# First attention: turning the probabilities with VectorE blocks and copies on the chip, in place of TensorE transposes

## The chip, the cores and the metric

The kernel runs on one core of one Trainium2 chip. The metric is the device time of one execution in microseconds. All five compute engines of the core run instruction streams of their own and meet at semaphores, written by hand.

## What is computed

Two blocks of a network run one behind the other on 256 tokens of 2048 features, all in float32. The first block has an attention layer with a relative bias (phase A), then one with forget gates (phase B), each with 32 heads of 128. The second block is a hybrid of convolution, sliding window attention and a recurrence, and the change does not touch it. The core of both phases, cut from the reference (bias, decay and masks in one name here):

```python
h = rms_norm(x, norm)
q, k, v, g = projections of h             # each 256 x 4096, 32 heads of 128
sc = einsum('bqhd,bkhd->bhqk', q, k) * scale + bias_or_decay_and_mask
p = softmax(sc)
o = einsum('bhqk,bkhd->bqhd', p, v)
x = x + (o * silu(g)) @ w_out
```

## The kernel before

**Tiling.** Tokens are taken in two halves of 128. Queries of the first half see the keys of the first half only (in both phases), queries of the second half see all 256 keys. So one head has 128x128 and 128x256 scores, 384 columns, and `scores` holds two heads: 128 partitions (queries) by 768. Two heads are a pair; each phase has 16 pairs, the first and the last written out, the 14 between in a loop.

**Weights.** Each product with a weight matrix goes in units of 256 columns: four units a pair (q, k, v, g), then 16 units for the output projection of the phase. A unit has four chunks (`PIECES`). SyncE loads a chunk of 512 KB to `w_raw` (`load_unit`, line 489), ScalarE rounds it to `w_hi` (`split_hi`, 685), VectorE makes the rest `w_lo` (`split_lo`, 1812), and TensorE multiplies with both (`multiply`, 1290; its matmuls are L1306 and L1308). `w_raw` and `w_both` each hold one unit. So SyncE may load a chunk when VectorE has split the same chunk of the unit before, ScalarE may split it when TensorE has used the same chunk of the unit before, and TensorE has three chunks to work through in between. Line 496 is the load, 689 the ScalarE split, 1814 the VectorE split.

**One pair,** in the order of TensorE (`pair`, 1356): unit k, unit v, the scores (1379, 1380), unit g, then six transposes (1387) of the finished probabilities into `ps_t`, the unit q of the next pair, and then `values(n)` (1394), which multiplies `v_tok` with the turned probabilities `p_t`. ScalarE copies `ps_t` to `p_t` (795). In the last pair of a phase `values` is not called there, but in the output projection, behind the first chunk of its first unit (`halves`, 1467, with `first_wait` at `s == 1`, 1474).

VectorE (`pair`, 1901) adds the bias to the scores (1921), splits chunk 0 of the next unit, takes the row maxima, splits chunk 1, waits for ScalarE's exponentials (784), scales by the reciprocal sums (1936, four instructions, then `p_ready`), and splits chunks 2 and 3. Further on it takes `g_t`, splits the next unit, takes `q_t` of the next pair (`take_scaled`) and multiplies the heads by the gate (`gate_heads`, 1958). In the last pair it splits parts of the gated heads in between (1896).

SyncE (`load_pair`, 511) loads the units in order, each chunk behind its wait, with one bias load (526) a pair ahead of unit v. In the second block it also makes copies from SBUF to SBUF (574, 585), all on the same queue.

The order on each engine is the order of the code. Nothing is planned by a tool.

Of the kernel before, what the change touches and what calls it, by code (L numbers as in the profile page):

```python
# [11 lines left out]
ACT = mybir.ActivationFunctionType  # L12
AX_X = mybir.AxisListType.X

P = 128
D = 2048
KT = D // P
S = 256
# [3 lines left out]
HEADS = INNER // P  # L22
PAIRS = HEADS // 2
UNIT_N = 256
PIECES = 4
PK = KT // PIECES
OUT_ORDER = ((0, 0), (0, 1), (0, 2), (1, 0), (0, 3), (1, 1), (1, 2), (1, 3))
QKVG = 4
OUT_N = D // UNIT_N
# [143 lines left out]
def build_program(nc, io, const_at):  # L173
    with ExitStack() as ctx:
# [3 lines left out]
        def sem(name):  # L178
            return ctx.enter_context(nc.semaphore(name))
# [7 lines left out]
        scratch = sb("scratch", [P, 18680])  # L187
# [3 lines left out]
        ps_s = ctx.enter_context(nc.psum_tensor("ps_s", [P, 2, 512], F32))  # L191
        ps_t = ctx.enter_context(nc.psum_tensor("ps_t", [P, 2, 512], F32))
        cum_dram = nc.dram_tensor("cumulative_log_forget", (HEADS, S), F32).ap()

        ident, ones = consts[:, 0:P], consts[:, P:2 * P]
# [8 lines left out]
        one = Region(scratch)  # L204
# [4 lines left out]
        bias_raw = one.take(2, S)  # L209
        bias = one.take(2, 384)  # L210
        scores = one.take(2, 384)
        p_t = one.take(2, 384)
        v_tok = one.take(2, S)
        tanh_g = one.take(2, S)
        sumsq = one.take(2, S)
# [8 lines left out]
        row_max = one.take(2, 2)  # L224
        row_sum = one.take(2, 2)

        before = p_t.rearrange("p a b -> p (a b)")
        vec_rows = before[:, 0:P]
        gate, gate_t, gate_u = (before[:, P + 2 * HEADS * n:P + 2 * HEADS * (n + 1)]
                                .rearrange("p (t h) -> p t h", t=2) for n in range(3))  # L230
        fw = og.rearrange("p h s -> p (h s)")[:, 3 * D:3 * D + KT * HEADS].rearrange("p (k h) -> p k h", k=KT)
        cum_row = bias.rearrange("p a b -> p (a b)")[0:HEADS, 0:S]
        squares = g_t
        first_squares = [g_t, v_t]
        z_rows = scores.rearrange("p a b -> p (a b)")[0:2 * HEADS, 0:2 * S]
# [72 lines left out]
        sides = [operand[:, n * SIDE:(n + 1) * SIDE].rearrange("p (k n) -> p k n", n=RAW_T) for n in range(4)]  # L308
# [53 lines left out]
        exp_done = sem("exp_done")  # L362
        recip_ready = sem("recip_ready")
        p_ready = sem("p_ready")
        turned = sem("turned")
        pt_ready = sem("pt_ready")
        tanh_done = sem("tanh_done")
        silu_ready = sem("silu_ready")
        o_done = sem("o_done")
# [100 lines left out]
        w_out_of = {"A": io["a_w_out"][0], "B": io["b_w_out"][0]}  # L470
# [15 lines left out]

        @block.sync
        def _(sp):
            def load_unit(unit, w, row0, column):

                for s in range(PIECES):

                    sp.wait_ge(pieces_split, unit * PIECES + s + 1)
                    rows = w[row0 + s * PK * P:row0 + (s + 1) * PK * P, :]
                    src = rows.rearrange("(k p) n -> p k n", p=P)[:, :, bass.ds(column, UNIT_N)]
                    sp.dma_start(w_raw[:, s], src).then_inc(raw_landed[s], 16)
# [11 lines left out]
            sp.dma_start(fw, io["f_w"].rearrange("(k p) n -> p k n", p=P)).then_inc(consts_in, 16)  # L508
            sp.dma_start(fb, io["f_b"].rearrange("(a n) -> a n", a=1).to_broadcast([P, HEADS])).then_inc(consts_in, 16)

            def load_pair(phase, i, last, first=False):
                unit = UNIT0[phase] + QKVG * i
                n = pair0[phase] + i

                if first:
                    load_unit(unit + 2, w_of[phase][2], 0, i * UNIT_N)
                    sp.wait_ge(cum_copied, 1)
                    sp.dma_start(cum_dram, cum_row).then_inc(cum_stored, 16)
                    sp.wait_ge(cum_stored, 16)
                sp.wait_ge(bias_ready, n + 1)  # L520
                if phase == "A":
                    rb = io["a_rel_bias"]
                    src = bass.AP(rb.tensor, rb.offset + 2 * i * REL + (REL - 2 * S + P), [[1, P], [REL, 2], [1, S]])
                else:
                    src = bass.AP(cum_dram.tensor, 2 * i * S, [[0, P], [S, 2], [1, S]])
                sp.dma_start(bias_raw, src).then_inc(bias_landed, 16)
                for c in (3,) if first else (2, 3):
                    load_unit(unit + c, w_of[phase][c], 0, i * UNIT_N)
                if not last:
                    for c in (0, 1):  # L530
                        load_unit(unit + QKVG + c, w_of[phase][c], 0, (i + 1) * UNIT_N)

            for phase in phases:
                if phase == "B":
                    for c in (0, 1):
                        load_unit(UNIT0[phase] + c, w_of[phase][c], 0, 0)
                load_pair(phase, 0, False, first=phase == "B")
                with sp.Fori(1, PAIRS - 1) as i:
                    load_pair(phase, i, False)
                load_pair(phase, PAIRS - 1, True)  # L540
                with sp.Fori(0, OUT_N) as j:
                    for half in range(2):
                        load_unit(UNIT0[phase] + UNITS_ATT + 2 * j + half, w_out_of[phase], half * D, j * UNIT_N)

# [136 lines left out]
        def _(act):  # L681
# [75 lines left out]
            def pair(phase, i, last, first=False):  # L757
                n = pair0[phase] + i
                unit = UNIT0[phase] + QKVG * i
                output = OUTPUT0[phase] + QKVG * i  # L760

                for s in range(PIECES):
                    split_hi(unit + 2, s)
                    if first and phase == "A" and s == 2:
                        root_of(0)
                copy_half(unit + 1, output + 1, 1)

                for s in range(PIECES):
                    split_hi(unit + 3, s)
                act.wait_ge(proj_free, output + 4)  # L770
                if first:
                    act.wait_ge(rstd_ready, phases.index(phase) + 1)
                scale_half_values(unit + 2, 0)

                if last:
                    gated_hi(pair0[phase], 0)
                split_hi(unit + 4, 0)
                if last:
                    gated_hi(pair0[phase], 1)
                split_hi(unit + 4, 1)  # L780
                act.wait_ge(negmax_ready, n + 1)
                for h in range(2):
                    for t, (a, b) in enumerate(((0, P), (P, 384))):
                        act.activation(scores[:, h, a:b], scores[:, h, a:b], ACT.Exp, bias=row_max[:, t, h:h + 1],
                                       accum_out=row_sum[:, t, h:h + 1]).then_inc(exp_done, 1)
                split_hi(unit + 4, 2)
                if last:
                    gated_hi(pair0[phase], 2)
                split_hi(unit + 4, 3)
                if last:  # L790
                    gated_hi(pair0[phase], 3)
                copy_half(unit + 3, output + 3, 1)

                act.wait_ge(turned, n + 1)
                act.activation(p_t, ps_t[:, :, 0:384], ACT.Copy).then_inc(pt_ready, 1)
                act.wait_ge(scaled, 3 * n + 3)
                act.activation(tanh_g, g_t, ACT.Tanh).then_inc(tanh_done, 1)
                if not last:
                    for s in range(PIECES):
                        split_hi(unit + 5, s)  # L800
                    copy_half(unit + 4, output + 4, 0)
# [485 lines left out]
        def _(pe):  # L1287
# [68 lines left out]
            def pair(phase, i, last, first=False):  # L1356
# [24 lines left out]
                m.then_inc(scores_done, 1)  # L1381
                multiply(unit + 3, 1, h_q)

                pe.wait_ge(p_ready, n + 1)
                for h in range(2):
                    for c in range(3):
                        m = pe.transpose(ps_t[:, h, c * P:(c + 1) * P], scores[:, h, (0, P, 2 * P)[c]:(0, P, 2 * P)[c] + P], ident)  # L1387
                m.then_inc(turned, 1)
                if not last:
                    pe.wait_ge(proj_free, output + 5)  # L1390
                    multiply(unit + 4, 0, h_q)
                    values(n)

            def values(n):
                pe.wait_ge(pt_ready, n + 1)
                for h in range(2):
                    pe.matmul(ps_s[:, h, 0:S], v_tok[:, h, 0:P], p_t[:, h, 0:S], start=True, stop=False)  # L1397
                    m = pe.matmul(ps_s[:, h, P:S], v_tok[:, h, P:S], p_t[:, h, S:384], start=False, stop=True)  # L1398
                m.then_inc(o_done, 1)

            def gates():
# [403 lines left out]
        def _(dve):  # L1805
# [6 lines left out]
            def split_lo(unit, s):  # L1812
                dve.wait_ge(hi_ready, unit * PIECES + s + 1)
                dve.tensor_tensor(w_lo[:, s], w_raw[:, s], w_hi[:, s].bitcast(F32), ALU.subtract).then_inc(pieces_split, 1)  # L1814
# [19 lines left out]
            def take_scaled(output, bank, dst, scale=1.0):  # L1834

                take_output(output, bank, dst)
                dve.wait_ge(proj_free, output + 3)
                scale_by_rstd(dst, scale)
# [62 lines left out]
            def pair(phase, i, last, first=False):  # L1901
# [32 lines left out]
                for h in range(2):  # L1934
                    for t, (a, b) in enumerate(((0, P), (P, 384))):
                        m = dve.tensor_scalar(scores[:, h, a:b], scores[:, h, a:b], row_sum[:, t, h:h + 1], None, ALU.mult)
                m.then_inc(p_ready, 1)
                if last:
                    gated_lo(phases.index(phase), 1)
                split_lo(unit + 4, 2)  # L1940
# [11 lines left out]
                if not last:  # L1952
                    for s in range(1, PIECES):
                        split_lo(unit + 5, s)
                    take_scaled(output + 4, 0, q_t, scale=SCALE)
                    gate_heads(n, 2 * i)

# [701 lines left out]
```

## Time and profile before

| | us |
|---|---|
| three runs, median | 2716.82 |
| lowest and highest | 2714.08, 2718.45 |
| span of the profiled execution | 2712.8 |

The profile is one execution with the times of each instruction. Busy time is the union of an engine's instructions; matmuls overlap each other, since they are pipelined. SPq is SyncE's queue of DMA issues, and the duration of a row there is the issue, not the movement of the data. PEclk is the clock that TensorE was granted, as a share of 2.4 GHz.

| engine | busy us | share |
|---|---|---|
| TensorE | 2692.7 | 99% |
| VectorE | 1810.4 | 67% |
| ScalarE | 1399.0 | 52% |
| GpSimd | 141.5 | 5% |

### The profile page before, as it was taken

To read this page: it belongs to the slowest core of one execution; us is meant where nothing else is said; L and a number is where in the kernel's file an instruction comes from. 1 tells how busy PE (TensorE), PEld (TensorE's weight loads), DVE (VectorE), ACT (ScalarE), POOL (GpSimd) and SP (SyncE) were. 2 spreads that over 40 slices of the span, in tenths; PEclk is the share of its full clock that TensorE was granted. 3 is DMA by queue.
4 is the path that set the end of the run, shared out by engine and by line. 5 is a ranking of instruction groups with operands and counts; after the bars stand their busy time and mean duration, and the time that the engine had idled before them with its cause. 6 is when DMAs were issued, how large, how long until landed. Compare 5 with 4: busy or idle time off the path is not lost.

```text
span 2712.8 us, 45296 instructions
## 1 busy us (share of the span) xinstructions
PE 2692.7 (99%) x17061; PEld 2415.2 (89%) x17061; DVE 1810.4 (67%) x2380; ACT 1399.0 (52%) x2132; POOL 141.5 (5%) x138
## 2 busy tenths in 40 slices
PE   8999999999999999999999999999999999999998
PEld 7888888888888888888888888888999999999987
DVE  7566565665665576565565656755889886689776
ACT  6444444444454454444444444544565774566764
POOL 0000000000000001001010010000000000000000
PEclk9999999999999999999999999999999999999999
DMA  7656666565556656565556565566554445564463
GB/s 228 184 177 184 178 181 177 179 185 175 178 177 191 188 160 184 176 181 178 178 181 182 178 180 177 176 191 188 182 170 147 133 153 172 166 184 149 133 208 127
DMA packets 474106, 475.94 MB, mean 175 GB/s; under 512 B 18090, under 2 KB 469058, under 8 KB 473730
## 3 DMA queue, kind: packets, MB, share of 16 engines
q1 hardware_dynamic: 473748, 474.35, 57.4%
q8 instruction: 70, 1.15, 0.2%
q14 instruction: 32, 0.26, 0.0%
q10 hardware_dynamic: 256, 0.18, 0.0%
HBM read 470.53 MB, written 2.13 MB: 174 GB/s over the span
## 4 chain that ended last, share of the span: by engine, by line
PE 93%; DVE 5%; ACT 1%; issue 1%; DMA 0%; SPq 0%; ACTq 0%; DVEq 0%
PE proj L1306 34%; PE proj L1308 17%; PE proj L1321 9%; PE proj L1493 6%; PE proj L1495 6%; PE proj L1494 6%; PE proj L1323 4%; PE proj L1715 2%; PE ps_s L1397 1%; DVE w_both L2152 1%; PE ps_s L1380 1%; DVE scratch L2311 1%; PE proj L1717 1%; PE ps_t L1387 1%; PE ps_s L1398 1%
## 5 line engine op out<-in xcount | busy, mean ns | idle before, releaser
L1306 PE MATMUL proj<-operand,w_both 128*128 128x512 f32 x3968 | 1402.5, 398 | 1.7 <-issue 1.2
L1814 DVE TENSOR_TENSOR w_both<-w_raw,w_both 128x1024 fp32r<-128x1024 f32 x644 | 799.4, 1244 | 694.1 <-ACT w_both L689 693.0
L689 ACT ACTIVATE w_both<-w_raw 128x1024 fp32r<-128x1024 f32 x644 | 681.8, 1059 | 916.7 <-PE proj L1308 704.4
L1308 PE MATMUL proj<-operand,w_both 128*128 128x256 f32 x4096 | 1143.4, 279 | 0.0
L1306 PEld LDWEIGHTS proj<-operand,w_both 128*128 128x128 f32 x3968 | 745.1, 188 | 175.5 <-issue 1.6
L1308 PEld LDWEIGHTS proj<-operand,w_both 128*128 128x128 f32 x4096 | 772.9, 189 | 0.8
L1493 PE MATMUL proj<-operand,w_both 128*128 128x272 f32 (+2 forms) x1540 | 448.6, 291 | 0.1
L1494 PE MATMUL proj<-operand,w_both 128*128 128x272 f32 (+2 forms) x1540 | 442.6, 287 | 0.0
L1495 PE MATMUL proj<-operand,w_both 128*128 128x272 f32 (+2 forms) x1540 | 442.4, 287 | 0.0
L1321 PE MATMUL proj<-w_both,operand 128*128 128x512 f32 x1024 | 363.2, 399 | 0.0
L2152 DVE TENSOR_TENSOR w_both<-w_raw,w_both 128x1024 fp32r<-128x1024 f32 x226 | 275.0, 1222 | 124.9 <-ACT w_both L902 124.0
L902 ACT ACTIVATE w_both<-w_raw 128x1024 fp32r<-128x1024 f32 x226 | 236.9, 1054 | 175.7 <-PE proj L1495 137.9
L1493 PEld LDWEIGHTS proj<-operand,w_both 128*128 128x128 f32 x1540 | 290.5, 189 | 5.7 <-issue 3.3
L1494 PEld LDWEIGHTS proj<-operand,w_both 128*128 128x128 f32 x1540 | 291.3, 189 | 0.3
L1495 PEld LDWEIGHTS proj<-operand,w_both 128*128 128x128 f32 x1540 | 291.4, 189 | 0.0
L1323 PE MATMUL proj<-w_both,operand 128*128 128x256 f32 x1024 | 287.6, 281 | 0.0
L1321 PEld LDWEIGHTS proj<-w_both,operand 128*128 128x128 f32 x1024 | 192.5, 188 | 47.7
L1323 PEld LDWEIGHTS proj<-w_both,operand 128*128 128x128 f32 x1024 | 193.7, 189 | 0.0
L2311 DVE SCALAR_TENSOR_TENSOR scratch<-scratch 128x272 f32<-128x272 f32 (+1 forms) x240 | 102.1, 487 | 0.8
L1715 PE MATMUL proj<-w_both,operand 128*128 128x512 f32 x224 | 79.4, 397 | 0.9 <-DVE w_both L2152 0.9
L1818 DVE TENSOR_TENSOR scratch<-proj,scratch 128x512 f32<-128x512 f32 x110 | 75.1, 683 | 0.1
L1831 DVE SCALAR_TENSOR_TENSOR scratch<-scratch 128x512 f32<-128x512 f32 x96 | 66.5, 693 | 3.3
(374 smaller groups left out, 2143.1 us busy)
## 6 DMA issues: line engine op xcount, KB each, us to landing
w_raw<-in_a_w_in_dram SPq DMA_DIRECT2D x256, 512.0 KB, 3.7
w_raw<-in_w_in_dram SPq DMA_DIRECT2D x160, 512.0 KB, 3.6
w_raw<-in_b_w_in_dram SPq DMA_DIRECT2D x128, 512.0 KB, 3.7
w_raw<-in_kv_w_dram SPq DMA_DIRECT2D x128, 512.0 KB, 3.8
w_raw<-in_a_w_out_dram SPq DMA_DIRECT2D x64, 512.0 KB, 4.6
w_raw<-in_b_w_out_dram SPq DMA_DIRECT2D x64, 512.0 KB, 4.1
w_raw<-in_w_out_dram SPq DMA_DIRECT2D x64, 512.0 KB, 3.6
scratch<-in_a_rel_bias_dram SPq DMA_DIRECT2D x16, 256.0 KB, 3.8
```

Of the source, the lines that this page charges most:

```text
L689: act.activation(w_hi[:, s], w_raw[:, s], ACT.Copy).then_inc(hi_ready, 1)
L902: act.activation(w_hi[:, s], w_raw[:, s], ACT.Copy).then_inc(hi_ready, 1)
L1306: pe.matmul(proj[:, 2 * bank + t, :], w_hi[:, s, kk, cols], rhs[:, k, :], start=first and k == 0, stop=False)
L1308: m = pe.matmul(proj[:, 2 * bank + t, 0:S], w_lo[:, s, kk, cols], rhs[:, k, 0:S], start=False, stop=last and end)
L1321: pe.matmul(proj[:, 2 * bank + t, :], hi, w_both[:, s, kk].rearrange("p a n -> p (a n)"), start=k == 0, stop=False)
L1323: m = pe.matmul(proj[:, 2 * bank + t, 0:UNIT_N], lo, w_hi[:, s, kk, :], start=False, stop=k == KT - 1)
L1493: pe.matmul(out, w_hi[:, s, kk, cols], hi, start=first, stop=False)
L1494: pe.matmul(out, w_hi[:, s, kk, cols], lo, start=False, stop=False)
L1495: return pe.matmul(out, w_lo[:, s, kk, cols], hi, start=False, stop=last)
L1715: pe.matmul(proj[:, bank + t, :], y[0][:, k, tokens], w_both[:, s, kk].rearrange("p a n -> p (a n)"), start=k == 0, stop=False)
L1814: dve.tensor_tensor(w_lo[:, s], w_raw[:, s], w_hi[:, s].bitcast(F32), ALU.subtract).then_inc(pieces_split, 1)
L2152: dve.tensor_tensor(w_lo[:, s], w_raw[:, s], w_hi[:, s].bitcast(F32), ALU.subtract).then_inc(pieces_split, 1)
```

## The change

The six transposes on TensorE and ScalarE's copy from PSUM go. VectorE turns the 128x768 probabilities in blocks of 32x32 (`p_blocks`, which lies on `q_t` and half of `k_t`, both read by then): a block stays in its own group of 32 partitions. Sixteen copies from SBUF to SBUF, of 32 partitions by 192 numbers (24 KB) each, move the blocks to the partitions of their keys (`p_keys`, in the place and size of `p_t`). They are issued by SyncE, eight ahead of the load of chunk 2 of the unit after the next pair's q and eight ahead of chunk 3. TensorE's `values` waits for all 16 to land and reads `p_keys` in runs of 32 numbers. VectorE waits for the same before it overwrites `q_t`. In the last pair of a phase the unit loaded among the copies is the second of the output projection, whose first two units move from the loop to here.

```diff
-        p_t = one.take(2, 384)
+        p_keys = one.take(4, 6, 32)
+        p_blocks = scratch[:, HEADS * S:HEADS * S + 768].rearrange("p (b c j) -> p b c j", b=4, c=6)
...
+            def move_blocks(n, sides):
+                sp.wait_ge(p_blocked, n + 1)
+                for b in sides:
+                    for a in range(4):
+                        sp.dma_start(p_keys[32 * b:32 * b + 32, a], p_blocks[32 * a:32 * a + 32, b]).then_inc(p_landed, 16)
...
-                if not last:
-                    for c in (0, 1):
-                        load_unit(unit + QKVG + c, w_of[phase][c], 0, (i + 1) * UNIT_N)
+                if last:
+                    following = [(w_out_of[phase], half * D, 0) for half in range(2)]
+                else:
+                    following = [(w_of[phase][c], 0, (i + 1) * UNIT_N) for c in range(2)]
+                load_unit(unit + QKVG, *following[0])
+                load_unit(unit + QKVG + 1, *following[1], chunks=(0, 1))
+                move_blocks(n, (0, 1))
+                load_unit(unit + QKVG + 1, *following[1], chunks=(2,))
+                move_blocks(n, (2, 3))
+                load_unit(unit + QKVG + 1, *following[1], chunks=(3,))
...
-                with sp.Fori(0, OUT_N) as j:
+                with sp.Fori(1, OUT_N) as j:
...
-                act.wait_ge(turned, n + 1)
-                act.activation(p_t, ps_t[:, :, 0:384], ACT.Copy).then_inc(pt_ready, 1)
...
-                pe.wait_ge(p_ready, n + 1)
-                for h in range(2):
-                    for c in range(3):
-                        m = pe.transpose(ps_t[:, h, c * P:(c + 1) * P], scores[:, h, (0, P, 2 * P)[c]:(0, P, 2 * P)[c] + P], ident)
-                m.then_inc(turned, 1)
...
-                pe.wait_ge(pt_ready, n + 1)
+                pe.wait_ge(p_landed, 256 * n + 256)
                 for h in range(2):
-                    pe.matmul(ps_s[:, h, 0:S], v_tok[:, h, 0:P], p_t[:, h, 0:S], start=True, stop=False)
-                    m = pe.matmul(ps_s[:, h, P:S], v_tok[:, h, P:S], p_t[:, h, S:384], start=False, stop=True)
+                    first = p_keys[:, :, 3 * h:3 * h + 2, :].rearrange("p a c j -> p c a j")
+                    second = p_keys[:, :, 3 * h + 2, :]
+                    pe.matmul(ps_s[:, h, 0:S].rearrange("p (c a j) -> p c a j", c=2, a=4), v_tok[:, h, 0:P], first, start=True, stop=False)
+                    m = pe.matmul(ps_s[:, h, P:S].rearrange("p (a j) -> p a j", a=4), v_tok[:, h, P:S], second, start=False, stop=True)
...
                 m.then_inc(p_ready, 1)
+                dve.wait_ge(p_ready, n + 1)
+                dve.transpose(p_blocks.rearrange("p b c j -> p c b j"),
+                              scores.rearrange("p h (c b j) -> p (h c) b j", c=3, b=4)).then_inc(p_blocked, 1)
...
                     for s in range(1, PIECES):
                         split_lo(unit + 5, s)
+                    dve.wait_ge(p_landed, 256 * n + 256)
                     take_scaled(output + 4, 0, q_t, scale=SCALE)
```

## Rows read from the trace of the kernel before

**Rows 1.** The page: span, TensorE's busy time, its granted clock in 40 slices.

```profile
span 2712.8 us, 45296 instructions
PE 2692.7 (99%) x17061; PEld 2415.2 (89%) x17061; DVE 1810.4 (67%) x2380; ACT 1399.0 (52%) x2132; POOL 141.5 (5%) x138
...
PEclk9999999999999999999999999999999999999999
```

**Rows 2.** TensorE's waits, whole span: total us, times, longest.

```profile
PE proj L1306 <- DVE w_both L1814: 0.5, 2, 0.3
```

**Rows 3.** TensorE in order of time, steady pair: start, us, line, operation.

```profile
544.61 0.28 PE L1308 MATMUL proj<-operand,w_both 128*128 128x256 f32 x1
544.73 0.82 PE L1387 MATMUL ps_t<-consts,scratch 128*128 128x128 f32 x6
...
545.62 0.28 PE L1308 MATMUL proj<-operand,w_both 128*128 128x256 f32 x1
...
545.97 0.28 PE L1308 MATMUL proj<-operand,w_both 128*128 128x256 f32 x1
```

**Rows 4.** The same, where `values` begins.

```profile
556.48 0.59 PE L1397 MATMUL ps_s<-scratch 128*128 128x256 f32 x2
```

**Rows 5.** VectorE in order of time, same pair; idle before and its releaser in brackets.

```profile
535.53 0.95 DVE L1921 TENSOR_TENSOR scratch<-ps_s,scratch 128x768 f32<-128x768 f32 x1
...
542.44 1.01 DVE L1936 TENSOR_SCALAR scratch<-scratch 128x128 f32<-128x128 f32 x4
...
546.02 1.23 DVE L1814 TENSOR_TENSOR w_both<-w_raw,w_both 128x1024 fp32r<-128x1024 f32 x1 [1.44 <-ACT w_both L689]
```

**Rows 6.** ScalarE in order of time, same pair.

```profile
539.38 1.06 ACT L689 ACTIVATE w_both<-w_raw 128x1024 fp32r<-128x1024 f32 x1 [1.71 <-PE proj L1308]
```

**Rows 7.** SyncE's queue of issues, same pair.

```profile
547.41 0.37 SPq L496 DMA_DIRECT2D w_raw<-in_a_w_in_dram  x1
```

**Rows 8.** Issues by line: count, duration ns min/median/max, first and last start.

```profile
L496 SPq DMA_DIRECT2D w_raw<-in_a_w_in_dram x256: 367/373/1721, 3.0 to 764.4; - x128
...
L574 SPq DMA_DIRECT2D scratch<-scratch x40: 624/625/917, 2005.7 to 2451.5; - x40
...
L585 SPq DMA_DIRECT2D scratch<-scratch x8: 607/628/718, 2031.0 to 2424.2; - x8
```

**Rows 9.** SyncE's queue in the second block, in order of time.

```profile
2033.74 0.60 SPq L562 DMA_DIRECT2D w_raw<-in_w_in_dram  x1
...
2045.97 2.94 SPq L574 DMA_DIRECT2D scratch<-scratch  x4
...
2059.52 2.65 SPq L574 DMA_DIRECT2D scratch<-scratch  x4
```

**Rows 10.** Stretches of 0.1 us; last two columns: DMA busy share, GB/s.

```profile
2049.50:2049.60 0.10, 0.10 (x3) 0.10 (x3) 0.10 (x1) 0.10 (x1) 0.00 (x0) 1.00 0.48 87
...
2049.80:2049.90 0.10, 0.10 (x3) 0.10 (x2) 0.10 (x2) 0.10 (x1) 0.00 (x0) 1.00 0.02 0
```

**Rows 11.** DMA issues of the page: size, median us from issue to landing.

```profile
w_raw<-in_a_w_in_dram SPq DMA_DIRECT2D x256, 512.0 KB, 3.7
...
scratch<-scratch SPq DMA_DIRECT2D x8, 136.0 KB, 4.0
...
cumulative_log_forget<-scratch SPq DMA_DIRECT2D x1, 32.0 KB, 1.9
```

**Rows 12.** VectorE and TensorE in order of time, last pair of phase A.

```profile
783.31 1.01 DVE L1936 TENSOR_SCALAR scratch<-scratch 128x128 f32<-128x128 f32 x4
...
789.14 0.67 PE L1397 MATMUL ps_s<-scratch 128*128 128x256 f32 x2
```

**Rows 13.** TensorE at the start in order of time; a stretch, clock third last.

```profile
6.87 1.92 PE L1352 MATMUL ps_t<-consts,scratch 128*128 128x128 f32 x8
...
11.52 1.04 PE L1352 MATMUL ps_t<-consts,scratch 128*128 128x128 f32 x8
...
2700.00:2705.00 5.00, 2.67 (x5) 0.55 (x3) 4.46 (x18) 0.80 (x3) 0.00 (x0) 0.57 0.36 132
```

More of the change, by code:

```diff
@@ L225, in build_program @@
         row_sum = one.take(2, 2)
-        before = p_t.rearrange("p a b -> p (a b)")
+        before = p_keys.rearrange("p a c j -> p (a c j)")
         vec_rows = before[:, 0:P]
@@ L364, in build_program @@
         p_ready = sem("p_ready")
-        turned = sem("turned")
-        pt_ready = sem("pt_ready")
+        p_blocked = sem("p_blocked")
+        p_landed = sem("p_landed")
         tanh_done = sem("tanh_done")
@@ L488, in _, with load_unit @@
         def _(sp):
-            def load_unit(unit, w, row0, column):
-                for s in range(PIECES):
+            def load_unit(unit, w, row0, column, chunks=range(PIECES)):
+                for s in chunks:
                     sp.wait_ge(pieces_split, unit * PIECES + s + 1)
```

## Prediction

> **What bounds the kernel now.** I read the page first: of a span of 2712.8 us TensorE is busy 99%, at a granted clock of nine tenths or more in every slice [rows 1]. Then TensorE's waits: in the matmul lines of the attention loops they come to half a microsecond in all [rows 2]. So TensorE sets the time, and an instruction taken from it is won, as long as nothing it needs comes later than before. Then one steady pair (of 16 in each of the two phases), in order of time, engine by engine, to find how late each input of TensorE may come. Then the queue of SyncE, because all 16 copies are put on it, and last the last pair of a phase, where the code puts `values(n)` elsewhere.
>
> **Removed from TensorE.** Six transposes a pair. Their busy time (0.82 us) overstates them, since matmuls overlap. From the L1308 that starts at 544.61 to the next at 545.62 there are 1.01 us, where two with no transposes between are 0.35 apart (545.62 and 545.97): 0.66 us a pair [rows 3]. Times 32: 21.1 us, 0.78% of the span. This is all that can be won.
>
> **Removed from ScalarE.** One copy of 128x768 a pair. ScalarE otherwise waits for TensorE to free weight buffers (1.71 us ahead of the split at 539.38 [rows 6]), so this is worth nothing.
>
> **Added to VectorE.** One 32x32 block transpose of 128x768 a pair, between the scaling of the probabilities, which starts at 542.44 and takes 1.01 [rows 5], and `split_lo` of chunk 2. No row shows a VectorE transpose. The nearest row of the same size, L1921 on 128x768, took 0.95 us [rows 5]; I take this. The scaling of the same columns in four instructions took 1.01. The ends are 0.7, a quarter less than the nearest row, and 1.9, two passes. The time itself is hidden: `split_lo` of chunk 3 starts only at 546.02, when ScalarE lets it, after 1.44 us of idleness [rows 5], and TensorE uses these chunks three chunks later, of 2.8 us each (from the end of the transposes, 545.3, to 556.48 there are four [rows 3, 4]). It counts only in the chain to `p_landed`.
>
> **Added to SyncE: the issues.** Sixteen copies of 24 KB from SBUF to SBUF. The kernel before has 48 issues of that kind, in the second block. They took 624 to 625 ns (minimum and median of 40, with 8 partitions and 17 KB) and 607 to 628 (of 8, with 64 partitions and 136 KB), against 373 for a weight load of 512 KB [rows 8]. The cost goes by the kind, not by the size, so I take it for 32 partitions too. Ten groups of four stand back to back, 2.65 to 2.94 us each [rows 9]; (2.65 - 0.62) / 3 = 0.675 from one start to the next. A weight load behind such copies took 0.60 instead of 0.37 [rows 9].
>
> **Added: the landing.** The fourth copy of the group at 2045.97 was issued at 2045.97 + 2.94 - 0.62 = 2048.29; after a still moment its packets run from 2049.5 and are gone by 2049.8 [rows 9, 10]. That is 1.5 us from the start of the issue, before the semaphore. The small store of `cum_dram`, 32 partitions and 32 KB, landed after 1.9; the 136 KB copies after 4.0, with weight loads around them [rows 11]. I take 1.8; the ends are 1.5 and 4.0. The last eight copies follow the load of chunk 2 by more than 5 us, so they should find an empty queue.
>
> A page of the Trainium skill, "DMA: Bandwidth & Descriptors", section "Anatomy of one DMA", gives a fixed 2.0 us and bytes/436 GB/s, for the GpSimd path: 2.06 us for 24 KB, an estimate by its figures. By it the sum below would be 0.26 x 32 = 8 us higher; the 1.9 us of the small store [rows 11] lie close to it, and no run here shows that landing for 24 KB; its rules for kernel authors also advise to coalesce anything under 64 KB, which this change does not do.
>
> **The steady pair, summed.** The scaling ends at 543.45; +0.03 allowed for VectorE's wait on its own semaphore, +0.95 transpose, +0.16 until SyncE issues (the split that starts at 546.02 and lasts 1.23 ends at 547.25, the load it releases starts at 547.41 [rows 5, 7]) = 544.59. Eight issues 7 x 0.675 + 0.62 = 5.35, with 0.10 for the first being longer and the gap; the load of chunk 2, 0.65 (its split has long ended); seven starts of 0.675 = 4.73: the last copy starts 10.83 later, at 555.42, and lands at 557.2. Before, `values` started at 556.48 [rows 4]; without transposes TensorE would be there at 555.82. It stands for 1.4 us, and the pair ends 0.77 later than before. The chain repeats in each pair, because its start hangs on TensorE: ScalarE's split at 539.38 was released by TensorE's use of chunk 1 of the same pair's last weight unit [rows 6]. Thirty pairs: +23 us.
>
> **The last pair of each phase.** Its `values` come after one chunk of output weights. Before, they started at 789.14, with the scaling starting at 783.31 and ending 1.01 later at 784.32 [rows 12]. By the same steps the copies land at 784.32 + 0.03 + 0.95 + 0.16 + 10.83 + 1.83 = 798.1, 9.0 us later. Two phases: +18 us. Nothing of this is hidden: the weights are ahead, and TensorE stands in front of them.
>
> **The clock.** Through the attention the page shows nine tenths or more, the 2.4 GHz level [rows 1]; in the closing stretch, where TensorE waits often, it reads 0.57 [rows 13]. At 6.87 us, with next to nothing done on TensorE before, eight transposes took 1.92 us, and eight of the same line 1.04 some 5 us later [rows 13], though the clock column there reads 1.0. So after a stop of 9 to 10 us I expect a few us at half the rate: 0 to 4 us a time, I take 2, so +4 us. After 1.4 us I expect nothing; no row in the loops shows such a stop.
>
> **Moved.** The load of chunk 2 of the following unit is issued some 5 us later (near 550), and chunk 3 at about 556.1, against 547.4 before [rows 7]; behind it wait the bias load and the first loads of the next unit. A weight load lands in about 3.7 us, so at 559.8; ScalarE splits it 3 us later than before, VectorE at about 561. TensorE, now in `values` until 558.5, needs it three chunks later, at 566.8. Some 4.5 us of cover are left; without it each microsecond would cost 32 us. VectorE's new wait for `p_landed` stands ahead of `take_scaled`, `gate_heads` and the next unit's splits; but the split of the late chunk 3, just ahead of it, ends at 562, so this wait comes for free, and `q_t` is not wanted before the next scores. `values` reads its moving operand in runs of 32 elements. No row shows that; with the same count of columns I take nothing (0 to 0.4 us a pair, the upper end if its two 256-column matmuls doubled).
>
> **Sum.** 23 + 18 + 4 = 45 us on the profiled span of 2712.8. That lies 4.0 us below the median of 2716.8 of the runs; the difference is carried along: 2762 us, +1.7%.
>
> **Rivals.** *Cheap issues (faster).* If a 32-partition copy costs what a load costs, 0.42 us from start to start with the gap, the chain from SyncE's first issue is 16 x 0.42 + 0.05 + 1.8 = 8.6 us, the copies land at 553.2, ahead of TensorE at 555.8, and every steady pair gains its 0.66: -20 us. The last pairs still cost 4.9 each, +10. Together -10, 2707 us. It decides below about 0.58 us a start; there the gain of the steady pairs just pays for the last ones. For it speak the issues of the far larger weight loads at 0.37, against it all 48 of the same kind [rows 8].
> *Late landing.* If the copies land after 4.0 us, like the 136 KB ones [rows 11], 2.2 x 32 = 70 us come on top: 2832 us. For it: it is the only landing shown for this kind; against: those were 8 packets an engine among weight loads, these are 2 or so.
> *A balance*, in which issues near 0.58 or two of these terms cancel: no change, 2717.
>
> Page "VectorE: DVE Perf Modes" of the Trainium skill, in "Rules for kernel authors", would give a 128x128 transpose to TensorE where PSUM will do, and calls VectorE fastest only inside 32x32. No time follows from it here; it leans to the slower side.
>
> **How the numbers follow.** Forecast 0.64, late landing 0.10, cheap issues 0.18, balance 0.08. About 0.2% (5 us) can be told from no change, so slower 0.74, same 0.08, faster 0.18. The forecast's own range: landing 1.5 to 2.4 (-10, +19), transpose 0.7 to 1.9 (-8, +30), clock (-4, +4), moving operand (+10 at most): 2740 to 2805. The range for 8 in 10 reaches down to 2706, to the cheap issues, and up to 2815, short of most of the late landing.
>
> **What would show it.** After: no L1387; TensorE idle ahead of the matmuls of `values` about 1.4 us, released by a DMA, 30 times, and about 9 to 10 us twice; SyncE's copies 0.62 us each, 0.675 apart; the last starting 10.8 us after the first. `w_both` waits of TensorE still near none. Wrong if the copies cost near 0.37, if the block transpose is not near 0.95, if TensorE waits for splits (then the moved loads count), or if the matmuls of `values` grow.

## The result and the profile after

The changed kernel takes 2735.6 us (median of 4 runs, 2734.1 to 2739.0) against 2715.7 of the kernel before: ratio 1.0074, 95% interval 1.0061 to 1.0086. The sign was forecast, the size was not: +20 us, not +45. The time lies inside the wide range (2706 to 2815), but below the forecast's own, 2740 to 2805. The span of the profiled execution grew by 22.4 us, from 2712.8 to 2735.2.

From the page of the changed kernel, first the span and the engines, then the chain that ended last:

```profile
span 2735.2 us, 45444 instructions
PE 2686.0 (98%) x16869; PEld 2401.2 (88%) x16869; DVE 1851.5 (68%) x2412; ACT 1378.1 (50%) x2100; POOL 137.3 (5%) x138
...
PE 78%; SPq 8%; DVE 7%; ACT 3%; issue 2%; DMA 2%; ACTq 0%; DVEq 0%
```

TensorE is busy 6.7 us less than before [rows 1], and the kernel is longer. SyncE's queue (SPq) stands in the chain with 8%, where it had nothing. TensorE's waits by line (total, times, longest) say what for; before, there was next to nothing in the attention [rows 2]:

```profile
PE ps_s L1407 <- DMA scratch<-scratch: 27.5, 22, 8.7
...
PE proj L1319 <- DVE w_both L1824: 2.1, 3, 1.7
```

L1407 is the first matmul of `values`. It waits 17.3 us of the 27.5 in two places, the last pairs of the phases, and 2.55 in the first pair. The three waits for split weights, 2.1 us, fall between 13 and 21 us, ahead of the attention's pairs, where the kernel before stops three times too (1.7 us). So the moved loads cost nothing on TensorE.

One steady pair of the changed kernel, in order of time on VectorE, SyncE and TensorE:

```profile
545.72 1.01 DVE L1946 TENSOR_SCALAR scratch<-scratch 128x128 f32<-128x128 f32 x4
546.77 0.98 DVE L1949 STREAM_TRANSPOSE scratch<-scratch 128x768 f32<-128x768 f32 x1
...
547.77 4.96 SPq L517 DMA_DIRECT2D scratch<-scratch  x8
553.00 0.37 SPq L497 DMA_DIRECT2D w_raw<-in_a_w_in_dram  x1
553.42 4.94 SPq L517 DMA_DIRECT2D scratch<-scratch  x8
558.62 0.38 SPq L497 DMA_DIRECT2D w_raw<-in_a_w_in_dram  x1
...
559.62 0.70 PE L1407 MATMUL ps_s<-scratch 128*128 128x256 f32 x2
```

The issues of the copies by their line (ns, minimum, median, maximum), and their landing:

```profile
L517 SPq DMA_DIRECT2D scratch<-scratch x512: 507/591/1513, 64.0 to 1766.1; - x171
...
DMA to landing us min/median/max: 1.7/1.8/3.4
```

The last copy is issued at 553.42 + 4.94 - 0.59 = 557.77 and lands 1.8 us later, at 559.57; `values` starts at 559.62.

**Where the 22.4 us are.** The reciprocal (L1932 before, L1942 after) comes once a pair, so its times measure pairs. Pairs 1 and 15 of phase A and 0 and 15 of phase B; first the kernel before, then the changed one:

```profile
108.89 0.18 DVE L1932 RECIPROCAL scratch<-scratch 128x4 f32<-128x4 f32 x1 [0.53 <-ACT scratch L784]
...
783.10 0.18 DVE L1932 RECIPROCAL scratch<-scratch 128x4 f32<-128x4 f32 x1 [0.53 <-ACT scratch L784]
...
1020.12 0.18 DVE L1932 RECIPROCAL scratch<-scratch 128x4 f32<-128x4 f32 x1 [0.53 <-ACT scratch L784]
...
1742.97 0.18 DVE L1932 RECIPROCAL scratch<-scratch 128x4 f32<-128x4 f32 x1 [0.53 <-ACT scratch L784]
```

```profile
112.49 0.18 DVE L1942 RECIPROCAL scratch<-scratch 128x4 f32<-128x4 f32 x1 [0.53 <-ACT scratch L799]
...
785.60 0.18 DVE L1942 RECIPROCAL scratch<-scratch 128x4 f32<-128x4 f32 x1 [0.53 <-ACT scratch L799]
...
1034.66 0.18 DVE L1942 RECIPROCAL scratch<-scratch 128x4 f32<-128x4 f32 x1 [0.53 <-ACT scratch L799]
...
1753.89 0.18 DVE L1942 RECIPROCAL scratch<-scratch 128x4 f32<-128x4 f32 x1 [0.53 <-ACT scratch L799]
```

| stretch | before | after | difference |
|---|---|---|---|
| start and first pair of A | 108.9 | 112.5 | +3.6 |
| 14 pairs of A | 674.2 (48.16 each) | 673.1 (48.08) | -1.1 |
| end of A to first pair of B | 237.0 | 249.1 | +12.0 |
| 15 pairs of B | 722.9 (48.19) | 719.2 (47.95) | -3.6 |
| from there to the end | 969.8 | 981.3 | +11.5 |

So the steady pairs gain a little, and the two ends cost 23.5 us.

A steady pair falls into two parts. From the reciprocal to the start of `values` the changed kernel takes 14.11 us in nearly every pair, whatever TensorE does: that is the chain through the copies. Before, it was 14.26 and 14.46 in turn, and where nothing waits it is 13.60 or 13.91. From `values` to the next reciprocal TensorE does not wait: 33.82 us in nearly every pair before, between 33.51 and 34.09 after. This second part moves with TensorE's own pace at the same clock (see the last section), not with the copies. So the copies account for a gain of about 0.25 us a steady pair, and the rest of the difference between steady pairs is pace.

At the end of phase A, `values` starts at 799.77, where it started at 789.14 [rows 12]; TensorE's clock by stretches (third last column):

```profile
799.77 1.19 PE L1407 MATMUL ps_s<-scratch 128*128 128x256 f32 x2 [8.64 <-DMA scratch<-scratch]
```

```profile
795.00:800.00 5.00, 0.23 (x1) 0.26 (x2) 1.92 (x2) 2.37 (x3) 0.00 (x0) 0.50 0.37 111
800.00:805.00 5.00, 5.00 (x16) 4.25 (x17) 1.82 (x2) 0.00 (x0) 0.00 (x0) 0.50 0.61 201
805.00:810.00 5.00, 5.00 (x31) 4.42 (x30) 2.16 (x2) 2.48 (x3) 0.00 (x0) 0.98 0.00 0
```

It has waited 8.64 us, and then works five more at the 1.2 GHz level, with 16 matmuls where the next stretch has 31. The clock falls a second time 180 us later, after a wait of only 1.09 us at 984.19 that both kernels have (1.15 before) and that left it alone before. The changed kernel, then the one before at the same work:

```profile
986.00:989.50 3.50, 3.50 (x12) 3.02 (x12) 3.47 (x8) 3.49 (x8) 0.00 (x0) 0.51 0.15 51
```

```profile
973.00:976.50 3.50, 3.50 (x22) 2.92 (x22) 3.47 (x8) 3.49 (x8) 0.00 (x0) 1.00 0.13 46
```

The same matmuls take 1.55 us longer there. It happens again from 2095.4 on, after a wait of 1.75 us (1.72 before), for 1.45 us. The first pair waits 2.55 us, because its exponentials come late and its first eight issues take 5.97 us instead of 4.96: one of them took 1.51. One issue in the loop's first pass took 1.50 too; in the last pairs of the phases, also written out, none did, so what makes an issue long is not shown.

### The profile page after: what moved, and what is told of

It reads as the page before. It is cut to its first block, busy times and chain, and to the rows that moved or that the text cites. A ratio compares the mean times of both kernels' runs of the same rounds, so it can differ in the third digit from the quotient of the medians.

```text
span 2735.2 us, 45444 instructions
## 1 busy us (share of the span) xinstructions
PE 2686.0 (98%) x16869; PEld 2401.2 (88%) x16869; DVE 1851.5 (68%) x2412; ACT 1378.1 (50%) x2100; POOL 137.3 (5%) x138
## 4 chain that ended last, share of the span: by engine, by line
PE 78%; SPq 8%; DVE 7%; ACT 3%; issue 2%; DMA 2%; ACTq 0%; DVEq 0%
PE proj L1319 24%; PE proj L1321 13%; PE proj L1334 9%; SPq L517 8%; PE proj L1503 6%; PE proj L1504 6%; PE proj L1505 6%; PE proj L1336 4%; PE proj L1725 2%; ACT scratch L799 2%; DMA scratch<-scratch 2%; PE ps_s L1407 1%; DVE w_both L2166 1%; PE ps_s L1393 1%; DVE scratch L2325 1%
## 5 line engine op out<-in xcount | busy, mean ns | idle before, releaser
L1841 DVE SCALAR_TENSOR_TENSOR scratch<-scratch 128x512 f32<-128x512 f32 x96 | 72.5, 755 | 3.3
```

## The experiments

Each kernel was timed beside the kernel before on its chip. The medians of the kernel before differ between sittings (2715.0 to 2720.7), so ratios are compared; 0.1% is 2.7 us. Pair lengths are from the reciprocals, as above.

### tail_te: is the loss at the ends of the phases?

```diff
 # TensorE, ScalarE: transposes and copy as before, if last
-                move_blocks(n, (0, 1))
+                if not last:
+                    move_blocks(n, (0, 1), phases.index(phase))
...
-                            values(pair0[phase] + PAIRS - 1)
+                            values(pair0[phase] + PAIRS - 1, r, turned_here=True)
```

> The changed kernel with one thing undone: in the last pair of each phase TensorE turns the probabilities again, and no copies are made there. Theory (a chain of 16 issues that TensorE waits for): each end of a phase cost 11.5 to 12 us in the changed kernel (8.6 and 8.7 us of waiting, and some 3 us at half the clock), so this kernel is 23 us below it: 2712 to 2714 us, within 0.2% of the kernel before. Rival (the cost is spread over all pairs, by late weight loads or by traffic): only a sixteenth of the 20 us comes back, 2734 us.

Measured: ratio 0.9975 (0.9964 to 0.9985), a span of 2712.2. The span is 23 us below that of the changed kernel, as the theory had it, and the spread-out rival is out. But the sum is right in part by luck: the two ends give back 17.7 us (249.1 becomes 239.9, 981.3 becomes 972.8), since TensorE ran the output projections of this kernel at a slower pace, about 3 us each (last section). The other 5.3 come from the start and the steady pairs, whose code is that of the changed kernel; its clock did not fall in the first pair, and more of its pairs ran at the faster pace.

### half_copies: does the number of issues decide?

```diff
-                move_blocks(n, (2, 3))
+                if phase == "A" and isinstance(i, int) and i == 0:
+                    move_blocks(n, (2, 3))
```

> Left out: from the second pair on, the eight copies to partitions 64 to 127, so the second half of the keys works with old numbers. The chain is 8 issues shorter, about 5.6 us. Theory: no steady pair waits any more, so each is 0.66 us shorter than before; the ends of the phases wait about 3 us instead of 8.7 and keep their clock or nearly. Against the kernel before: 28 x -0.66 = -18, ends 2 x (3 - 0.7) = +5, first pair +4, together -9: 2707 us. Rival (the price is that of moved loads or of the block transposes on VectorE, which stay as they are): near the changed kernel, 2730 or more.

Measured: 0.9954 (0.9938 to 0.9971), a span of 2707.0, and every pair after the second at 47.42 us. Its waits for copies:

```profile
PE ps_s L1408 <- DMA scratch<-scratch: 8.7, 3, 3.2
```

Three waits are left, the first pair and the two ends. VectorE's transpose and the copies' place in the queue are as in the changed kernel, so they are not the price.

### unwaited: is anything else paid?

```diff
-                        sp.dma_start(p_keys[32 * b:32 * b + 32, a], ...).then_inc(p_landed, 16)
+                        sp.dma_start(p_spare[32 * b:32 * b + 32, a], ...).then_inc(p_landed, 16)
 # TensorE transposes and works with p_t, as before
```

> Everything that the change adds, and nothing that it removes: VectorE turns the blocks, SyncE makes the 16 copies at the same places (to a spare region), but TensorE still transposes and works with what ScalarE copied from PSUM. TensorE waits for no copy. Theory: all other costs are hidden, so the time is that of the kernel before, 2716 us, or up to 3 us more for the first pairs, whose loads are latest. Rival (moved loads, traffic, VectorE's longer row of work): at least 10 us more than before.

Measured: 0.9993 (0.9983 to 1.0002), a span of 2712.9, pairs of 48.19 and 48.18 us, as before. All that the change adds is hidden, so long as nobody waits for it: the block transpose, 512 issues, the copies' traffic and the late loads.

### shapes: why did an issue take 0.59 and not 0.625?

```diff
+    # phase A, to a spare region; src on q_t and k_t
+    sp.dma_start(dst[to:to + 32, 0:192], src[of:of + 32, 0:192])
+    sp.dma_start(dst[to:to + 8, 192:384], src[of:of + 8, 0:192])
+    sp.dma_start(dst[to:to + 32, 384:928], src[of:of + 32, 0:544])
+    sp.dma_start(dst[to:to + 32, 928:1120], two runs of 96 of src)
```

> TensorE's part is that of the kernel before; nobody waits for the copies, which go to a spare region and serve only to measure the issue. In phase A each group has four forms, one line each: 32 partitions by 192 numbers; 8 by 192; 32 by 544; 32 by two runs of 96. In phase B: 32 by 96; 16 by 192; 32 by 512; 32 by 192. The forecast took 0.625 us an issue from copies of 8 partitions by 544 numbers and 64 partitions by two runs of 272; the copies of the change took 0.591. If the kind alone sets the cost, all forms take 0.59. If long rows cost more, 32 by 544 takes 0.625 and the others 0.59. If two runs cost more, that form alone. If few partitions cost more, 8 and 16 by 192 do.

Measured in one run of 2716.1 us (a span of 2714.3, close to the kernel before), in this order of lines, then 32 by 96, 16 by 192, 32 by 512 and 32 by 192 in phase B:

```profile
L524 SPq DMA_DIRECT2D scratch<-scratch x64: 544/588/622, 64.1 to 793.5; - x64
L525 SPq DMA_DIRECT2D scratch<-scratch x64: 662/670/740, 64.8 to 794.2; - x64
L526 SPq DMA_DIRECT2D scratch<-scratch x64: 513/518/1201, 65.5 to 794.9; - x64
L527 SPq DMA_DIRECT2D scratch<-scratch x64: 636/641/1217, 66.1 to 795.4; - x64
L529 SPq DMA_DIRECT2D scratch<-scratch x64: 511/584/597, 1022.2 to 1753.9; - x64
L530 SPq DMA_DIRECT2D scratch<-scratch x64: 586/591/1352, 1022.9 to 1754.6; - x64
L531 SPq DMA_DIRECT2D scratch<-scratch x64: 589/589/597, 1023.5 to 1755.2; - x64
L532 SPq DMA_DIRECT2D scratch<-scratch x64: 590/591/1364, 1024.1 to 1755.8; - x64
```

None of the four guesses holds alone. Eight partitions cost 0.08 us more than 32, sixteen nothing; two runs cost 0.05 more in this place; 544 numbers cost 0.07 less, where 512 cost nothing less. The forecast's rows were copies of 8 partitions by 544, and of 64 partitions in two runs: they differ from 32 by 192 in the very things that moved the price here. For the form of the change, 0.59 is right in both phases. The forms stood in a fixed order, so what a neighbour does to an issue isn't told apart.

### two_runs: does the row of issues set the steady pair?

```diff
-        p_blocks = ....rearrange("p (b c j) -> p b c j", b=4, c=6)
+        p_blocks = ....rearrange("p (h b c j) -> p h b c j", h=2, b=4, c=3)
 # two transposes, one a head; each copy reads two runs of 96
```

> The changed kernel, but the blocks lie so that each copy reads two runs of 96 numbers a partition instead of one of 192. Same bytes, same partitions, same 16 copies. By the kernel of shapes such an issue takes 0.641 us against 0.588 to 0.591. VectorE turns each head by itself (two instructions, some 0.1 us more). Theory (the steady pair waits for the end of the row of issues, so 15 x 0.05 = 0.8 us and 0.1 to 0.2 for the transpose come through in full): 28 to 30 pairs by 0.9 us are +27 us, the ends +2: 2764 us, which is where the forecast had the change, with 0.675 from start to start. Rival (the steady pair of the changed kernel is balanced by something else, such as the weight loads): 2736 to 2745 us.

Measured: 1.0099 (1.0083 to 1.0116), a span of 2747.7. That is 12 us above the changed kernel in span, about 7 by the ratios, and not 28.

```profile
550.44 5.10 SPq L517 DMA_DIRECT2D scratch<-scratch  x8
```

```profile
L517 SPq DMA_DIRECT2D scratch<-scratch x512: 588/597/1515, 64.3 to 1776.7; - x171
```

The issue took 0.597 in this company, not 0.641: from start to start (5.10 - 0.60) / 7 = 0.643 against (4.96 - 0.59) / 7 = 0.624. Fifteen times 0.019 is 0.29, the two transposes add 0.06 and the landing 0.04: 0.39 us of chain. From the reciprocal to `values` it measured 14.47 us instead of 14.11, so 0.36 more. Pairs grew by 0.32 in A (48.40) and 0.36 in B (48.31). So the pair follows the chain one for one, and the rival is out although the time, 2748 us, lies nearer to its range than to the 2764 expected: the size of the step was wrong, because 0.641 did not carry over from one place to another.

### loads_last: the same from the other side

```diff
-                load_unit(unit + QKVG + 1, *following[1], chunks=(2,))
                 move_blocks(n, (2, 3))
+                load_unit(unit + QKVG + 1, *following[1], chunks=(2,))
```

> The changed kernel with the load of chunk 2 behind all 16 copies instead of between them. The row of issues to the last copy gets 0.67 us shorter, the load is issued 5 us later. Theory: the steady pairs stop waiting but for little, down from about 48.0 to 47.5, 28 x -0.5 = -14 us, the ends -1.3, together 2720 us, if the cover of the weight load holds. Rival (the loads are already as late as they can be): TensorE now waits for splits in every pair, and nothing is gained or time is lost, 2736 us or more.

Measured: 0.9999 (0.9990 to 1.0009), a span of 2713.8, pairs of 47.44 and 47.42 us. One weight load out of the row, 0.67 us, and the steady pair stops waiting; TensorE meets no late split, though chunk 2 is issued some 5 us later. The load had cover to spare.

### two_queues: two rows side by side

```diff
 # SyncE
-                move_blocks(n, (2, 3))
 # ScalarE
+                act.wait_ge(p_blocked, n + 1)
+                for b in (2, 3):
+                    for a in range(4):
+                        act.dma_start(p_keys[32 * b:32 * b + 32, a], ...).then_inc(p_landed_act, 16)
                 act.wait_ge(scaled, 3 * n + 3)
```

> The changed kernel with eight of the 16 copies issued by ScalarE, at the place where its copy from PSUM was, and eight by SyncE. The chain then has two parallel parts of 5 us. Theory (what counts is the number of issues in a row on one queue): the blocks have landed some 4 us earlier, no steady pair waits, 47.42 us each (-21 us over all); at the ends the copies land at about 794.5 where values could start at 788.5, a wait of 6 us and some clock, +8 us each. Together 2716 - 21 + 16 = 2711 us. Rival (the issues of both queues are made by one unit, one after the other): nothing gained against the changed kernel, 2736 us, or more, since ScalarE's splits now stand behind them.

Measured: 0.9978 (0.9967 to 0.9989), a span of 2714.2. TensorE's waits for copies are the two ends (9.7 us in all, 5.9 the longest); issues on ScalarE's queue took 0.612 us, on SyncE's 0.592. So the queues issue side by side, and the rival is out. Pairs are 47.42 in B but 47.84 in A, without a wait; the difference is TensorE's pace (last section).

### bounce: through DRAM, in five issues

```diff
-                move_blocks(n, (0, 1))
+                sp.wait_ge(p_blocked, n + 1)
+                sp.dma_start(p_dram, p_blocks.rearrange("p b c j -> p b (c j)")).then_inc(p_stored, 16)
                 load_unit(unit + QKVG + 1, *following[1], chunks=(2,))
-                move_blocks(n, (2, 3))
+                sp.wait_ge(p_stored, 16 * n + 16)
+                for b in range(4):
+                    sp.dma_start(p_keys[32 * b:32 * b + 32].rearrange("i a c j -> i a (c j)"),
+                                 p_dram[:, b].rearrange("(a i) n -> i a n", a=4)).then_inc(p_landed, 16)
```

> The 16 copies are replaced by one store of all blocks to DRAM and, behind the load of chunk 2, four fetches, which pick the blocks of all source groups at once. Chain by the rows of the kernel before: store landed after about 2.3 us, four fetches at 0.42 from start to start, landing 3.7 after the issue: about 7.7 us against 11.9 of the 16 copies. Theory: steady pairs no longer wait (-0.66 each, 28 of them: -18), the ends wait about 4.5 us instead of 8.7 with less loss of clock: 2 x (4 - 0.7 + 1) = +9, first pair 0 to +2. Together -8: 2708 us, 1% below the changed kernel. Rival (the round trip through DRAM is as slow as the 16 copies, since its landings stand behind weight loads): 2730 to 2740.

Measured: 0.9952 (0.9935 to 0.9969), a span of 2710.8, all pairs from the third on at 47.42 us. Store and fetches land after 2.4 and 3.3 us, but are five issues. The ends still wait 4.9 and 5.0 us.

### bounce_tail: both together

The edits of bounce, and those of tail_te.

> The store to DRAM and four fetches in place of the 16 copies, in all pairs but the last of each phase, where TensorE turns the probabilities as in the kernel before. Theory: no TensorE wait for copies is left anywhere. The pairs run at 47.42 us against 48.18 of the kernel before, 28 to 29 times: -21 us, and the ends of the phases cost nothing: 2716 - 21 = 2695 us, 0.8% below the kernel before. Rival (part of the loss at the ends is not the waiting but the loads that moved from the loop into the last pair): 2700 us or more.

Measured: 2692.2 us, ratio 0.9921 (0.9904 to 0.9938), a span of 2689.8. No wait for copies is left. It beats both kernels: 0.8% below the kernel before, 1.5% below the changed one. One steady pair on SyncE:

```profile
536.85 0.35 SPq L518 DMA_DIRECT2D turned_blocks<-scratch  x1
538.09 0.37 SPq L500 DMA_DIRECT2D w_raw<-in_a_w_in_dram  x1
539.20 1.76 SPq L524 DMA_DIRECT2D scratch<-turned_blocks  x4
```

The last fetch starts at 540.5 and lands about 544, where the 16 copies took 11.8 us from the first issue to the last landing; `values` comes at 548.5.

## Why the forecast was right and wrong

**TensorE's gain, 0.66 us a pair: close.** A pair without transposes and without waits takes 47.42 us (half_copies, bounce, bounce_tail). Before, pairs took 48.08 and 48.29 in turn: 0.66 and 0.87 more. The transposes cost 0.66. The other 0.21 is TensorE's pace: the 121 close steps from one L1306 to the next take 42.35 us in the pair from 253.13 and 42.56 in the one from 301.21.

**Block transpose, 0.95 us: right** (0.978, 32 times). **Landing, 1.8 us: right.** The Trainium skill's "DMA: Bandwidth & Descriptors", "Anatomy of one DMA", would give 2.06 us for 24 KB (an estimate by its figures), for another issuing path; here the trace shows 1.8, and the measurement decides. **`values` in runs of 32, nothing: right.** From its start to the next matmul of the projection it takes 1.23 us in bounce and half_copies, as in the kernel before.

**Issues, 0.675 us from start to start: too much, and this is the step that failed.** It was 0.624, which makes 14 x 0.051 = 0.7 us a pair. SyncE's start after the transpose was another 0.14 too late in the forecast (0.02 instead of 0.16), the allowance of 0.10 for a longer first issue fell away. So the copies landed 11.8 us after the first issue, not 12.6. The forecast had `values` 0.77 us later than before in each pair; 0.77 - 0.7 - 0.14 - 0.10 is -0.2. Measured from the reciprocal, the forecast had `values` at 15.02 us (557.25 against 542.23) and it came at 14.11, ahead of the 14.26 and 14.46 of before. The pairs came out 0.08 and 0.24 shorter on average, with TensorE's pace mixed in. Thirty pairs turned from +23 us to -5. The sum stood on a balance: the copies land nearly when TensorE arrives, and each 0.1 us in the row of issues is 3 us of kernel. two_runs and loads_last show this from both sides, +0.34 and -0.58 us a pair for a chain 0.36 longer and 0.67 shorter (the latter down to the floor of 47.42). The rows that I took the price from were of the right kind, but not of the right form, and the range of the issue price was never written down: 0.675 had one value in the sum, while landing and transpose had two ends; a lower price stood only in the rival, at 0.42.

**The last pairs, +18: right in mechanism,** `values` started 8.1 us later after the reciprocal at both ends, where 9.0 was forecast: +16 us. **The clock, +4: too little.** The ends of the phases cost 12.0 and 11.5 us, 3 to 4 each above that. In A, `values` took 2.56 us instead of 1.30 in the stretch at the 1.2 GHz level, and the five matmul pairs behind it 3.12 instead of 1.81, 2.6 us together; the second fall, from 986.1 on, cost 1.55. In B it was 1.5 us behind the wait and 1.45 from 2095.4 on. Together some 7 us, and nearly half of it came long after the waits, at places that the forecast did not look at; that the change itself brings these later falls about is not shown, since the same wait left the clock alone in loads_last, which makes the same copies.

**The first pair: not in the sum.** +3.6 us: `values` starts 2.05 us later after the reciprocal (2.55 of waiting), and then the clock falls for 3.4 us, which costs most of the rest. The forecast counted it as steady, though its issue and its exponentials both come late.

**Cover of the moved loads: right.** ScalarE now waits for the weight loads of the attention for 278.5 us in all, where it was 1.9, and TensorE has no wait for splits in the pairs. unwaited shows that the late loads and the added traffic are free while nobody waits for the copies.

**Rivals.** Cheap issues, decided at "about 0.58 us a start" for the whole kernel: the measured 0.624 lies above, and the kernel was slower, but the steady pairs alone had crossed their own point. Late landing: did not happen.

## What to carry to other kernels

When work leaves the bounding engine for a queue of many small transfers, count the issues in a row, not the bytes, and set their end against the moment of use; then do it again for each place where the consumer comes early, here two pairs in 32, which cost more than the 30 others gave. Here five issues through DRAM beat 16 on the chip, and the last pair of each phase, written out by itself, did best the old way. Take the price of an issue from the same form of transfer, or carry a range for it, above all where the sum lands near a balance.

## What was not expected of the hardware

**The clock after short stops.** It fell after 8.6, 5.9, 4.9 and 3.8 us of waiting (the ends of the phases in the changed kernel, bounce and two_queues), and also in the first pair of the changed kernel, where TensorE had waited 2.55 us from 74.4 on:

```profile
76.00:78.00 2.00, 1.07 (x6) 1.00 (x7) 0.64 (x1) 0.00 (x0) 0.00 (x0) 1.00 0.47 113
78.00:80.00 2.00, 2.00 (x9) 1.78 (x8) 0.00 (x0) 0.11 (x1) 0.00 (x0) 0.53 0.99 269
```

In half_copies it did not fall after 3.17 us (the wait ends at 784.8), and did fall after 3.20 at the same place of phase B (the wait ends at 1738.4):

```profile
785.00:789.00 4.00, 4.00 (x25) 3.53 (x25) 3.04 (x5) 2.53 (x3) 0.00 (x0) 1.00 0.74 256
```

```profile
1739.00:1742.00 3.00, 3.00 (x12) 2.63 (x11) 2.05 (x4) 2.52 (x3) 0.00 (x0) 0.50 0.86 298
```

In the first pair it fell after 2.52 us in two_runs and not after 2.52 in tail_te. Between the phases, after a wait of 1.06 to 1.15 us that all kernels have, it fell in the changed kernel, two_runs, two_queues and bounce, and in none of the others. So in these runs the length of a stop alone does not tell whether the clock falls; what does is not shown.

**TensorE's pace at the same clock.** In the loop of the output projection, the same matmuls in the same order run at 0.347 us a pair of matmuls in some places and at 0.353 in others, at a granted clock of 1.00 and without waits. The changed kernel, then bounce:

```profile
859.88 0.39 PE L1319 MATMUL proj<-operand,w_both 128*128 128x512 f32 x1
...
861.96 0.39 PE L1319 MATMUL proj<-operand,w_both 128*128 128x512 f32 x1
```

```profile
859.72 0.40 PE L1326 MATMUL proj<-operand,w_both 128*128 128x512 f32 x1
...
861.84 0.40 PE L1326 MATMUL proj<-operand,w_both 128*128 128x512 f32 x1
```

Six pairs in 2.08 and in 2.12 us. In phase A, slow there were bounce, half_copies, two_queues and tail_te; fast were the others. In phase B two_queues was fast and two_runs slow, so it is no property of a whole program. The end of phase A took 239.9 us in tail_te and 236.9 in bounce_tail, both without a wait of note in it; the pace accounts for that. In the attention both paces stand in one pair, and how much runs at each changes from pair to pair: that is the 0.21 us between the pairs of the kernel before, and the 0.42 between two_queues' pairs of phase A and B (123 close steps take 43.47 and 43.05 us). What sets the pace I don't know; no experiment changed it on purpose. Differences of 0.1% between such kernels should not be read as an effect of the edit.

**Issue price.** An issue of 544 numbers a partition cost 0.518 us, one of 512 cost 0.589 and one of 96 cost 0.584. More bytes were cheaper to issue, in one place of one kernel.
